# Head 0's experts are chosen eight and eight, sums start ahead of the second head's choice, and one tile's rows are shifted by ACT and DVE together

## What is computed

```python
x = x + mod_x[2] * merge_branches(...)            # 256 x 1024, in tiles t = 0, 1
h = modulate(rmsnorm(x, norm2_g), mod_x[3], mod_x[4])
q = (h @ peer_wq).reshape(128, 8, 2, 128)         # per tile: 8 heads, two halves
s = jnp.einsum('chpd,hpkd->chpk', q, peer_keys)   # two scores lists of 128 per head
sv, si = lax.top_k(s, 16)
cand = sv[..., 0, :, None] + sv[..., 1, None, :]  # 16 x 16 sums of pairs
cidx = si[..., 0, :, None] * 128 + si[..., 1, None, :]
top_s, pos = lax.top_k(cand, 16)                  # 16 experts of a head
eidx = take_along_axis(cidx, pos); gate = softmax(top_s)
act = gelu(einsum('chkd,cd->chk', peer_u[eidx], h))
x = x + mod_x[5] * einsum('chk,chkd->cd', gate * act, peer_v[eidx])
```

## Time and profile before

| | us |
|---|---|
| median of 3 runs | 2640.28 |
| lowest and highest | 2638.99, 2640.45 |
| the profiled execution's own time | 2640.01 |
| its span | 2638.1 |

### The profile page before, as it was taken

The page is one execution under the profiler, slowest core; times in us unless marked ns, Lnnn a source line. Parts: engine busy times, 40 slices in busy tenths (PEclk is TensorE's granted clock), DMA queues, the critical chain, the costliest instruction groups (busy, mean ns, idle before and its releaser), DMA issues.

```text
span 2638.1 us, 48116 instructions
## 1 busy us (share of the span) xinstructions
PE 2438.0 (92%) x19036; PEld 1682.9 (64%) x19036; DVE 1509.2 (57%) x2848; ACT 899.9 (34%) x2505; POOL 649.6 (25%) x512
## 2 busy tenths in 40 slices
PE   8999999999999999999999888989999987877787
PEld 6588696476887954845677778888865532322232
DVE  1874376537734755576457445455056666677654
ACT  1252100013330000016332333221016676766676
POOL 0000014300000242000014657440013454444551
PEclk9999999999999999999999999999999999999999
DMA  4432444344234545215432111003449999999997
GB/s 186 156 128 97 160 160 160 147 175 150 106 124 180 224 160 206 114 64 224 158 130 64 34 23 30 19 34 137 159 181 393 414 421 421 421 422 421 421 421 301
DMA packets 91686, 523.98 MB, mean 199 GB/s; under 512 B 39776, under 2 KB 39776, under 8 KB 43488
## 3 DMA queue, kind: packets, MB, share of 16 engines
q0 software_dynamic: 39360, 277.51, 25.7%
q1 hardware_dynamic: 52128, 243.80, 24.8%
HBM read 511.85 MB, written 9.44 MB: 198 GB/s over the span
## 4 chain that ended last, share of the span: by engine, by line
PE 68%; DVE 11%; DMA 10%; issue 5%; ACT 3%; POOL 1%; POOLq 1%; DVEq 1%; ACTq 1%; PEldq 0%; SPq 0%
PE psum L571 34%; PE psum L1890 23%; DMA mem<-weights,mem 10%; PE psum L2379 5%; DVE mem L2780 4%; DVE mem L3324 3%; PE psum L813 2%; PE psum L587 1%; POOL mem L3378 1%; PE psum L2347 1%; DVE mem L3131 1%; PE psum L1900 1%; POOLq L3435 1%; ACT mem L2724 0%; ACT mem L2720 0%
## 5 line engine op out<-in xcount | busy, mean ns | idle before, releaser
L1890 PE MATMUL psum<-mem 64*64 64x64 f32 (+6 forms) x12356 | 874.4, 265 | 53.9 <-DVEq L3135 14.7
L571 PE MATMUL psum<-mem 128*128 128x128 f32 (+9 forms) x4856 | 910.4, 359 | 11.2 <-DVE mem L1198 3.5
L1890 PEld LDWEIGHTS psum<-mem 64*64 64x64 f32 (+4 forms) x12356 | 710.3, 151 | 208.1 <-issue 124.5
L571 PEld LDWEIGHTS psum<-mem 128*128 128x128 f32 (+4 forms) x4856 | 685.4, 183 | 230.5 <-issue 158.1
L2379 PE MATMUL psum<-mem 128*128 128x512 f32 x1024 | 505.3, 633 | 108.2 <-ACT mem L2724 108.0
L2379 PEld LDWEIGHTS psum<-mem 128*128 128x128 f32 x1024 | 187.5, 197 | 419.4 <-ACT mem L2724 259.2
L3324 DVE CUSTOM_DVE_ANT_0 mem<-mem 128x1024 f32<-128x1024 f32 x256 | 314.1, 1227 | 208.0 <-DMA mem<-weights,mem 191.3
L3484 POOL DMA_INDIRECT mem<-weights,mem x256 | 295.1, 1153 | 537.1 <-PE psum L2379 310.3
L2780 DVE TENSOR_TENSOR mem<-psum,mem 128x512 f32<-128x512 f32 (+2 forms) x180 | 111.5, 630 | 254.8 <-PE psum L1890 228.2
L3378 POOL TENSOR_TENSOR mem<-mem 128x512 f32<-128x512 f32 (+3 forms) x148 | 205.7, 1402 | 153.7 <-DVEq L3100 120.2
L2780 DVE TENSOR_TENSOR mem<-mem 128x512 f32<-128x512 f32 (+4 forms) x154 | 135.4, 893 | 11.8 <-ACTq L2540 2.2
(11 more groups left out here) (284 smaller groups left out, 1791.9 us busy)
## 6 DMA issues: line engine op xcount, KB each, us to landing
mem<-weights SPq DMA_DIRECT2D x97, 2048.0 KB, 7.3
mem<-weights SPq DMA_DIRECT2D x13, 1024.0 KB, 9.9
rates_dram<-mem POOLq DMA_DIRECT2D x16, 512.0 KB, 5.0
mem<-rates_dram SPq DMA_DIRECT2D x32, 256.0 KB, 4.6
mem<-weights SPq DMA_DIRECT2D x2, 2176.0 KB, 7.9
mem<-weights,mem POOLq DMA_INDIRECT x256, 30.8
mem<-weights SPq DMA_DIRECT2D x2, 1536.0 KB, 8.1
mem<-weights SPq DMA_DIRECT2D x2, 1152.0 KB, 8.8
```

Source lines behind the costliest of these rows:

```text
L571: ins = pe.matmul(out, lhsT, rhs, start=start, stop=stop, skip_group_check=skip)
L1890: ins = pe.matmul(out, lhsT, rhs, start=start, stop=stop, skip_group_check=skip)
```

## The change

1. `tile_evac(0)` on ACT does four of the eight pieces; DVE does the other four (`first_tile_evac`), and PE waits for both.
2. Unit 0 is chosen in two steps. `first_eight` takes the eight best of each list, their 8 x 8 sums and the best eight of these; `second_eight` the rest. POOL starts slot 0 behind the first step and waits for the second at slot 8.
3. On DVE the dots of groups 0 and 1 stand between the steps of unit 1's choice; unit 2's steps move by one group.
4. On PE the sums of a group stand between the pieces of query work: group 0 ahead of the wq1 queries of tile 1, group 1 ahead of the key scores, group 4 ahead of h2's transposes, and `query_chunk(2, c)` is followed by group 5 + c in place of 4 + c. The wq0 queries of tile 1 come in two halves.
5. ACT follows that order up to group 5; its list behind it is as before. The exponential of unit 1 moves behind the key scores' copies.
6. Buffers 6 and 7 move to places 3 and 4 of the cycle of eight, so that slots 11 and 12 use them first (before: slots 8 and 9).

```diff
-    first_bufs = [*range(5), 8, 9, 5, 6, 7] + [*range(8)] * 4 + [8, 9, *range(8)] * 2
+    eight = [0, 1, 2, 6, 7, 3, 4, 5]
+    first_bufs = [*range(5), 8, 9, 5] + eight * 4 + [8, 9, *eight] * 2
-    cycle = [*range(8, 16), *range(8)]
+    cycle = [*range(8, 16), *eight]
@@ PE
         pe.wait_ge(*hT2_by_act.at(0, 2))
+        pe.wait_ge(*hT2_by_dve.at(0, 2))
...
         tile_queries(wq1, 0)
         tile_transposes(1)
+        sums([0])
         pe.wait_ge(*hT2_by_act.at(0, 3))
         tile_queries(wq1, 1)
+        sums([1])
         key_scores(1)
-        sums([0, 1, 2])
-        tile_queries(wq0, 1)
+        sums([2])
+        tile_queries(wq0, 1, (0, 1))
         sums([3])
+        tile_queries(wq0, 1, (2, 3))
+        sums([4])
         key_scores(0, (1,))
         h2_transposes(1)
         pe.drain().then_inc(weights.used, 1)
         for c in range(4):
             query_chunk(2, c)
-            sums([4 + c])
+            sums([5 + c])
         key_scores(2)
         for c in range(4):
             query_chunk(3, c)
-            sums([8 + c])
+            sums([9 + c])
         key_scores(3)
-        sums(range(12, len(SLOT_GROUPS)))
+        sums(range(13, len(SLOT_GROUPS)))
@@ ACT
         def tile_evac(t):
-            for q in range(2):
+            for q in range(2 if t else 1):
...
         tile_evac(1)
+        slot_weights([0])
+        tile_queries(1, 1)
+        slot_weights([1])
+        key_scores(1)
         expert_gates(1)
-        tile_queries(1, 1)
-        slot_weights([0])
-        key_scores(1)
-        slot_weights([1, 2])
-        tile_queries(0, 1)
+        slot_weights([2])
+        tile_queries(0, 1, 0, 2)
         slot_weights([3])
+        tile_queries(0, 1, 2, 4)
+        slot_weights([4])
         key_scores(0, (1,))
         h2_copies(1)
-        slot_weights([4, 5])
+        slot_weights([5])
         query_pair(2, 0)
         slot_weights([6, 7])
         query_pair(2, 1)
@@ DVE
+        def first_tile_evac():
+            b = act_ring.peek(v, "post", "hT", 1)
+            for c in range(4):
+                k = 4 + c
+                last = v.tensor_scalar(hT[:, k, 0:P], b[:, c * P:(c + 1) * P], AB[:, 4, k:k + 1], AB[:, 5, k:k + 1], ALU.mult, ALU.add)
+            last.then_inc(act_ring.free, 1)
+            v.drain().then_inc(hT2_by_dve.sem, 1)
+        def first_eight():
+            v.wait_ge(*scores_ready.at(0, SCORED[0, 0]))
+            for c in range(2):
+                v.max(sv[:, 0, c, 0:8], sp_[:, 0, c, :])
...
+            choose_eight(0, 8)
+        def second_eight():
+            for c in range(2):
+                v.match_replace(sp_[:, 0, c, :], sv[:, 0, c, 0:8], sp_[:, 0, c, :], -3e38)
...
+            choose_eight(8, 16)
...
         tile_norm(0)
+        first_tile_evac()
         add_out(1, 0)
-        choose_first(0)
+        first_eight()
+        second_eight()
         add_out(1, 1)
         tile_norm(1)
-        choose_first(1)
+        rank(1)
         expert_gates(0)
+        v.wait_ge(*h2_ready.at(0, 0))
+        slot_dots(0)
+        pair_up(1)
+        rank_pairs(1)
+        slot_dots(1)
+        choose(1)
         expert_gates(1)
-        v.wait_ge(*h2_ready.at(0, 0))
-        for b in range(len(SLOT_GROUPS)):
+        for b in range(2, len(SLOT_GROUPS)):
@@ POOL
-            if n in UNIT_AT:
-                pool.wait_ge(*experts_ready.at(0, UNIT_AT[n]))
+            if n in (0, 8):
+                pool.wait_ge(*experts_ready.at(0, n // 8))
+            elif n in UNIT_AT:
+                pool.wait_ge(*experts_ready.at(0, UNIT_AT[n] + 1))
```

More of the change, by code:

```diff
@@ L2679, in tile_evac @@
                 done(last)
+            if t == 0:
+                act_ring.held(1, "hT")
             act.drain().then_inc(hT2_by_act.sem, 1)
@@ L2729, in slot_weights @@
                     slot_weight(n)
-                if b % 8 == 3 and b // 8 + 2 < len(UNITS):
+                if b % 8 == (3 if b >= 8 else 5) and b // 8 + 2 < len(UNITS):
                     expert_gates(b // 8 + 2)
@@ new lines, in look_up_eight, with choose_eight @@
+        def look_up_eight(s, width, src, dst):
+            e3 = eqb[:, 0:8 * width].rearrange("p (k n) -> p k n", n=width)
+            tt(e3, bc(src, 2, width), bc(C2["iota16"][:, 0:width], 1, 8), ALU.is_equal)
+            v.drain()
+            tt(e3, e3, bc(sif[:, 0, s, 0:width], 1, 8), ALU.mult)
+            v.drain()
+            v.tensor_reduce(dst, e3, AX.X, ALU.add)
+            v.drain()
+        def choose_eight(first, width):
+            pu = posu_u[:, 0, 0, first:first + 8]
+            v.tensor_scalar(hiu_u[:, 0:8], pu, 4, None, ALU.logical_shift_right)
+            v.tensor_scalar(lou_u[:, 0:8], pu, 15, None, ALU.bitwise_and)
+            v.drain()
+            v.tensor_copy(hif[:, 0:8], hiu_u[:, 0:8])
+            v.tensor_copy(lof[:, 0:8], lou_u[:, 0:8])
+            v.drain()
+            look_up_eight(0, width, hif[:, 0:8], i1f[:, 0:8])
+            look_up_eight(1, width, lof[:, 0:8], i2f[:, 0:8])
+            v.scalar_tensor_tensor(i1f[:, 0:8], i1f[:, 0:8], float(P), i2f[:, 0:8], ALU.mult, ALU.add)
+            v.drain()
+            v.tensor_copy(eidx_u[:, first:first + 8], i1f[:, 0:8]).then_inc(experts_ready.sem, 1)
@@ new lines, in second_eight @@
+        def second_eight():
+            for c in range(2):
+                v.match_replace(sp_[:, 0, c, :], sv[:, 0, c, 0:8], sp_[:, 0, c, :], -3e38)
+            v.match_replace(head0[:, 0:P], tops[:, 0, 0, 0:8], head0[:, 0:P], -3e38)
+            v.drain()
+            for c in range(2):
+                v.max(sv[:, 0, c, 8:16], sp_[:, 0, c, :])
+            v.drain()
+            for c in range(2):
+                v.max_index(siu_u[:, 0, c, 8:16], sv[:, 0, c, 8:16], sp_[:, 0, c, :])
+            tt(grid[:, 0:8, 8:16], bc(sv[:, 0, 0, 0:8], 2, 8), bc(sv[:, 0, 1, 8:16], 1, 8), ALU.add)
+            tt(grid[:, 8:16, :], bc(sv[:, 0, 0, 8:16], 2, 16), bc(sv[:, 0, 1, :], 1, 8), ALU.add)
+            v.drain()
+            v.tensor_copy(sif[:, 0, 0:2, 8:16], siu_u[:, 0, 0:2, 8:16])
+            v.max(tops[:, 0, 0, 8:16], head0)
+            v.drain()
+            v.max_index(posu_u[:, 0, 0, 8:16], tops[:, 0, 0, 8:16], head0)
+            v.drain()
+            choose_eight(8, 16)
+            y = tops[:, 0, 0:1, :]
+            tt(gatep[:, 0, 0:1, :], y, bc(y[:, :, 0], 2, 16), ALU.subtract)
+            v.drain().then_inc(gate_shift_ready.sem, 1)
@@ L3357, in _ @@
             if ahead < len(UNITS):
-                phase = b % 8 - (ahead == 2)
+                phase = b % 8 - (2 if ahead == 2 else 0)
                 if phase == 0:
@@ L3365, in _ @@
                     choose(ahead)
[L3366 removed]
+                elif phase == 4:
                     expert_gates(ahead)
@@ L3472, in _ @@
                 pool.wait_ge(*hT2_by_act.at(0, 3))
-            for g, done in ((1, 3), (3, 6)):
+            for g, done in ((1, 3), (3, 7)):
                 if m is None and at == behind_query[g][0]:
```

23 lines of the change are left out of this document (15 added, 8 removed).

## The result

| | before | changed kernel |
|---|---|---|
| median (6 runs each, side by side) | 2640.36 us | 2668.5 us |
| lowest and highest | 2636.09, 2641.76 | 2663.63, 2677.79 |
| ratio, 95% interval | | 1.011 [1.0092, 1.0128] |

The forecast was 2667, with a range of 2654 to 2681. The profiled execution of the changed kernel is the slowest of its six: 2677.79 us, with a span of 2675.9.

What follows compares the result with a forecast made beforehand. The end was set by when the first gather is issued and how long its queue runs dry, with the buffer loop binding. 20.9 us at slot 58 plus 5.7 of PE clock made 26.6, forecast 2667 us, range 2654 to 2681.

Steps and rivals of the forecast that it cites:

- The first eight: Head 0's choice on DVE: first eight experts ready at 1954.6, so the first gather goes out 5.1 us earlier.
- The chain of groups: PE and ACT in the new order, each waiting for the other: group 5 ends at 2053.5, group 9 at 2109.7.
- The waits on PE: PE waits 6.1, 4.8 and 5.4 us ahead of groups 0, 2 and 9, and seven times about 2.5.
- Slot 58: Gather 58 waits for slot 48's buffer and lands at 2148.0 against 2127.1, +20.9 us; the 501 us after stay the same.
- Clock: PE's clock drops behind long waits, costing 1.9 us each, 5.7 in all; rival that every wait costs: 2680, chance 0.10.
- the three long waits: PE's waits ahead of groups 0, 2 and 9, charged 5.7 us together for lower clock.
- none of the seven: PE's seven waits of about 2.5 us were charged no lost clock.
- Holes: DMA was to run dry at about 1987 to 1992, 2022, 2036, 2052, and some 5 us near 2108.
- ACT's idle time ahead of wq1's copy: ACT was to stand idle from 1978.8 to 1988.1, about 9 us, before copying wq1's tile 1 queries.
- The restart price: A gather issued into an empty queue takes 6.1 us to its dot; used for gather 58.
- The estimate of 4.4: Skill page's 4.4 us for a gather where rows show 6.1; it would make the sum 1.7 us less, 2665.

Runs made afterwards that it cites:

- e_order: The changed kernel with head 0's experts again chosen in one piece, its orders, buffers and shift kept: 26.7 us slower than the kernel before.
- e_eights: The kernel before with only head 0's experts chosen in two eights: ratio 1.0007 to the kernel before, medians -0.2 us.
- e_best2: The kernel before with groups, dots, choices and exponentials re-placed, tile 0's shift on two engines, and head 0 chosen in two eights: 3.1 us faster than before.
- e_again: The changed kernel unchanged, run and profiled once more: 26.5 us slower than the kernel before.
- e_queries_first: The changed kernel with wq1's tile 1 queries ahead of group 0 on PE, their copy ahead of group 0's weights on ACT: 22.8 us slower than before.
- the late stage: The kernel before with only group 4 ahead of head 0's key scores and h2 transposes, and chunks followed by groups 5+c and 9+c: 18.6 us slower.
- e_late_queries: The changed kernel, late stage undone, PE's wq1 queries ahead of group 0, wq0's ahead of group 3, unit 2's exponential moved back: 3.0 us slower than before.

## Why the prediction was right, step by step

- **The first eight** came as forecast: the first gather 5.17 us earlier than before, counted from the transposes (15.53 against 20.70; forecast 5.1). That this is lost was right too (e_order, e_eights, e_best2).
- **The chain of groups.** Counted from the first gather, PE ends group 0 at 27.6 us in e_again (1981.02 less 1953.47), where the chain had 25.9; group 2 at 61.6 (58.0), group 8 at 140.9 (136.6), group 9 at 160.6 (154.8). The differences are 1.7, 3.6, 4.3 and 5.8. Long sums take 1.55 to 1.59 us over 7.78 at groups 0, 2 and 9; with those up to each point taken out 0.1, 0.5, 1.1 and 1.1 are left. So the chain is right to 1.1 us over 160. The waits on PE came as forecast too: 6.21, 5.16 and 5.17 us ahead of groups 0, 2 and 9, and seven of 2.62 to 2.84.
- **Slot 58.** In e_again its dot starts 27.4 us later than before, counted from the transposes (215.17 against 187.77); forecast 20.9 + 5.7 = 26.6. Without the clock it is 22.7 against 20.9. From it to the last dot 502.2 us; forecast 501, 501.1.
- **Clock.** The size was near and the rule half right. In e_again exactly the three long waits cost, 4.7 us together (forecast 5.7). In the slower execution groups 1 and 3 are long as well, behind waits of 2.84 and 2.63, and the five cost 9.4 us over 7.78 each. That is 4.6 more, and its last dot is 4.5 us later than e_again's. So "none of the seven" was a choice that holds in one execution and not in the next. The two profiled executions differ by this and by the 6.2 us between their starts of the transposes; both are likely sources of the 14 us among the six runs, of which only one was profiled. The Trainium skill (TensorE: Matmul & The Clock Gate, HAM oscillation) has a burst start throttled behind each wait that is long enough. The trace agrees behind each wait above 5 us; group 8, behind 2.84, ran at 7.78 in both executions.
- **How near the number is.** 1.5 us between forecast and median is closer than the terms allow, and in part luck: the chain was 1.8 us short up to slot 58 and 1.1 behind it, and the clock was 1.0 too dear in one execution and 3.7 too cheap in the other.
- **Holes.** Four of the five are there, one is not, and others were not named. In e_again, whose first gather goes out 1.4 us ahead of the forecast's, the first lies at 1986 to 1992, the fourth of the list (2052, here some 2050) is missing, and the one near 2108 lies at 2103 to 2111. The holes named at 2022 and 2036 are those ahead of gathers 20 and 24 (issued at 2023.56 and 2037.55); ahead of gather 16 (2010.31) there is one more, which the list left out. Two later ones, ahead of gathers 50 and 58 (shares of 0.27 at 2121 to 2124 and 0.44 at 2146 to 2150), were not named either. Windows of e_again, the third with no hole:

```profile
2009.00:2013.00 4.00, 4.00 (x9) 1.72 (x8) 3.85 (x27) 2.14 (x8) 1.89 (x2) 0.84 0.30 72
2036.00:2042.00 6.00, 5.77 (x13) 1.96 (x13) 4.93 (x8) 4.34 (x16) 3.39 (x3) 1.00 0.40 124
2049.00:2055.00 6.00, 6.00 (x15) 2.47 (x14) 1.23 (x2) 4.47 (x17) 2.87 (x3) 1.00 1.00 429
2103.00:2111.00 8.00, 6.27 (x10) 2.73 (x11) 7.33 (x20) 6.43 (x23) 1.01 (x2) 0.61 0.19 57
```

ACT's idle time ahead of wq1's copy was 10.8 us in e_again against 9.3 forecast; 1.6 of it is group 0's clock. Ahead of the other copies of queries it was 5.4 to 8.1 us, as the 5 to 8 forecast.

- **The restart price.** Gather 58, issued just as the queue ran dry (a share of 0.20 to 0.28 in that half microsecond), took 5.7 and 6.3 us to its dot (2157.59 to 2163.26, 2146.81 to 2153.11), as the row's 6.1. The estimate of 4.4 from the Trainium skill (DMA: Bandwidth & Descriptors, anatomy of one DMA) is short for this gather in each.
- **Where the text was wrong.** It followed one chain from the first group to slot 58 and left unsaid which links carry the loss. A reader would take the first waits for the costly ones, since the first is the longest. The runs show that undoing it moves the last dot by 1 us (e_queries_first), while the late stage makes 18.6 of 26.2 us. And a single link, the rank that stands one group too early for its scores, is worth 8.

## What to carry to other kernels

Where two engines hand work to each other in written order, an item moved ahead on one of them must be moved on the other too, together with everything that stands behind it and has another source; look for the instruction whose input comes from the group just ahead of it (here the rank behind group 8). An earlier start of a queue that is fed from few buffers is worth only what the buffers' return allows: price it at the first request that needs a buffer back. And count the banks of a shared ring before copies are moved behind other work. When one part of a change is undone to price it, look in the trace for a wait that neither neighbour had: in e_late_queries such a wait, 10.96 us on ACT, is enough to spoil the price.
